# Where the operands of TensorE start in SBUF: stationary buffers on multiples of 64 bytes, ring slots 16 bytes further apart

## The reference

```python
h = x + 0.5 * swiglu(norm(x), w_ffn1_in, w_ffn1_out)         # d_ff 5632
z = norm(h) @ w_mix_in                                        # 5 groups of 1024 columns: B, C, H, U, V
y_conv = B * causal_dwconv3(C * H)
y_gm   = U * (tril(w_spatial[head]) @ norm(V) + b_spatial)
h = h + concat(y_conv, y_gm) @ w_mix_out
h = h + cross_attention(norm(h), norm(mem), w_xq, w_xk, w_xv, w_xo)   # 4 heads, 256 memory tokens
h = h + 0.5 * swiglu(norm(h), w_ffn2_in, w_ffn2_out)
out = norm(h)
```

## Time and profile before

| what | value |
|---|---|
| median of three runs | 2189.96 us |
| profiled execution, span from first to last instruction | 2187.2 us |
| TensorE busy with matmuls | 2167.1 us, 99% |
| VectorE busy | 1349.3 us, 62% |
| ScalarE busy | 991.6 us, 45% |
| DMA from and to HBM | mean 188 GB/s |

### The profile page before, as it was taken

One profiled execution on the slowest core, in us unless ns is written; L12 is line 12 of the kernel. 1 busy time (PEld: TensorE's weight loads), 2 busy tenths in 40 slices (PEclk: granted clock), 3 DMA queues, 4 the chain that ended last, 5 costly groups with the idle time before them and its releaser, 6 DMA issues.

```text
span 2187.2 us, 25558 instructions
## 1 busy us (share of the span) xinstructions
PE 2167.1 (99%) x9626; PEld 1778.9 (81%) x9626; DVE 1349.3 (62%) x1549; ACT 991.6 (45%) x1103; POOL 1.8 (0%) x7
## 2 busy tenths in 40 slices
PE   8999999999999999999999999999999999999998
PEld 6888888888888888888888888888888888888886
DVE  5676667666474547865677554576676667664544
ACT  5444454444343444444554444454444444443433
POOL 0000000000000000000000000000000000000000
PEclk9999999999999999999999999999999999999999
DMA  6666666665556565665556445466666666665553
GB/s 227 209 190 197 195 191 188 197 195 189 188 171 204 181 191 181 195 227 175 180 170 207 155 159 169 157 212 197 193 191 193 192 192 190 195 194 187 188 188 135
DMA packets 159217, 412.20 MB, mean 188 GB/s; under 512 B 12588, under 2 KB 13732, under 8 KB 158756
## 3 DMA queue, kind: packets, MB, share of 16 engines
q1 hardware_dynamic: 157728, 410.04, 60.2%
q10 hardware_dynamic: 1412, 1.11, 0.2%
HBM read 409.01 MB, written 2.10 MB: 188 GB/s over the span
## 4 chain that ended last, share of the span: by engine, by line
PE 96%; DVE 2%; ACT 1%; DMA 0%; issue 0%; ACTq 0%; DVEq 0%
PE ps L906 94%; PE ps L935 1%; DVE w_lo L575 1%; PE ps L919 1%; DVE ps L635 1%; DVE convT L748 0%; DVE xT_lo L583 0%; DMA h<-in_x 0%; ACT convT L444 0%; PE ps L1023 0%; ACT xT_hi L329 0%; ACT w_hi L321 0%; DVE stage L738 0%; ACT scratch L555 0%; ACT zT L441 0%
## 5 line engine op out<-in xcount | busy, mean ns | idle before, releaser
L575 DVE TENSOR_TENSOR w_lo<-raw,w_hi 128x1024 fp32r<-128x1024 f32 x768 | 936.1, 1224 | 773.8 <-ACT w_hi L321 768.6
L321 ACT ACTIVATE w_hi<-raw 128x1024 fp32r<-128x1024 f32 x768 | 811.8, 1061 | 1106.0 <-PE ps L906 1087.0
L906 PE MATMUL ps<-w_hi,xT_hi 128*128 128x512 f32 x1856 | 573.8, 390 | 5.3 <-DVE w_lo L575 5.3
L906 PE MATMUL ps<-w_lo,xT_hi 128*128 128x512 f32 x1856 | 572.2, 389 | 0.0
L906 PE MATMUL ps<-w_hi,xT_lo 128*128 128x512 f32 x1856 | 572.0, 389 | 0.0
L906 PEld LDWEIGHTS ps<-w_hi,xT_hi 128*128 128x128 f32 x1856 | 347.8, 188 | 78.9 <-issue 4.1
L906 PEld LDWEIGHTS ps<-w_lo,xT_hi 128*128 128x128 f32 x1856 | 349.0, 188 | 72.7
L906 PEld LDWEIGHTS ps<-w_hi,xT_lo 128*128 128x128 f32 x1856 | 348.7, 188 | 72.8
L906 PE MATMUL ps<-w_hi,hidT_hi 128*128 128x512 f32 x704 | 223.5, 397 | 0.4 <-DVE w_lo L575 0.4
L906 PE MATMUL ps<-w_hi,hidT_lo 128*128 128x512 f32 x704 | 222.7, 395 | 0.0
L906 PE MATMUL ps<-w_lo,hidT_hi 128*128 128x512 f32 x704 | 221.3, 393 | 0.0
(11 more groups left out here) (119 smaller groups left out, 800.7 us busy)
## 6 DMA issues: line engine op xcount, KB each, us to landing
raw<-in_w_ffn_in SPq DMA_DIRECT2D x352, 512.0 KB, 4.1
raw<-in_w_ffn_out SPq DMA_DIRECT2D x176, 512.0 KB, 4.3
raw<-in_w_mix_in SPq DMA_DIRECT2D x80, 512.0 KB, 4.2
raw<-in_w_mix_out SPq DMA_DIRECT2D x32, 512.0 KB, 3.7
raw<-in_w_xq SPq DMA_DIRECT2D x32, 512.0 KB, 3.8
raw<-in_w_xk SPq DMA_DIRECT2D x32, 512.0 KB, 3.9
raw<-in_w_xv SPq DMA_DIRECT2D x32, 512.0 KB, 3.6
raw<-in_w_xo SPq DMA_DIRECT2D x32, 512.0 KB, 3.6
```

The source lines that it names most:

```text
L321: nc.scalar.activation(w_hi[:, k % RING, :], raw[:, k % RAW, :], ACT.Copy).then_inc(hi_ready, 1)
L575: nc.vector.tensor_tensor(w_lo[:, k % RING, :], raw[:, k % RAW, :], w_hi[:, k % RING, :].bitcast(F32), ALU.subtract).then_inc(lo_ready, 1)
L906: ins = nc.tensor.matmul(bank(s, t * GW + b * BLK, BLK), xs[:, k, t * P:(t + 1) * P], ws_[:, k % RING, b * BLK:(b + 1) * BLK], start=(k == ...
```

## The change

`put` takes a `row`: the tensor then starts at a byte that is 64 * `row` past a multiple of 512. `xT_hi` gets row 0 and `xT_lo` row 4. `extra` is rounded up to a multiple of 64, and with it everything that lies on `extra` and `big`. The rings `w_hi` and `w_lo` become one flat tensor each, in which a slot is 1024 columns and the next slot starts 1028 columns (4112 bytes) further: `w_hi` starts on row 0, `w_lo` on row 4. The three places that use a slot take `w_hi[k % RING]` instead of `w_hi[:, k % RING, :]`.

| tensor | start before: byte, remainder by 64, by 512 | start after |
|---|---|---|
| `xT_hi` | 32896, 0, 128 | 33280, 0, 0 |
| `xT_lo` | 49280, 0, 128 | 49920, 0, 256 |
| `w_hi` slots 0 to 3 | remainders 0, 0, 0, 0 by 64 | 0, 16, 32, 48 by 64 |
| `w_lo` slots 0 to 3 | remainders 0, 0, 0, 0 by 64 | 0, 16, 32, 48 by 64 |
| `hidT_hi`, `yT_hi` | 137504, 32, 288 | 138752, 0, 0 |
| `pT_hi` | 129312, 32, 288 | 130560, 0, 0 |
| `v_hi` | 203040, 32, 288 | 204288, 0, 0 |

The instructions of every engine, their order and their waits stay as they are; only addresses differ.

```diff
--- before.py
+++ after.py
@@ -103,21 +103,33 @@
     KB = 1024
     place = {"at": BASE}
 
-    def put(name, shape, dt, at=None):
+    LINE = 64
+    PITCH = 512
+
+    def lines(at, row):
+        return at + (row * LINE - at) % PITCH
+
+    def put(name, shape, dt, at=None, row=None):
         size = 4
         for s in shape[1:]:
             size *= s
         if at is None:
-            at = place["at"]
-            place["at"] = at + (size + 31) // 32 * 32
+            at = (place["at"] + 31) // 32 * 32
+            if row is not None:
+                at = lines(at, row)
+            place["at"] = at + size
         return nc.alloc_sbuf_tensor_at(name, shape, dt, offset=at)
 
+    def put_ring(name, dt, skew, row):
+        ring = put(name, [P, RING * (GW + skew)], dt, row=row)
+        return [ring[:, i * (GW + skew):i * (GW + skew) + GW] for i in range(RING)]
+
     h = put("h", [P, TOK, D], F32)
-    xT_hi = put("xT_hi", [P, KD, SEQ], F32R)
-    xT_lo = put("xT_lo", [P, KD, SEQ], F32R)
+    xT_hi = put("xT_hi", [P, KD, SEQ], F32R, row=0)
+    xT_lo = put("xT_lo", [P, KD, SEQ], F32R, row=4)
     raw = put("raw", [P, RAW, GW], F32)
-    w_hi = put("w_hi", [P, RING, GW], F32R)
-    w_lo = put("w_lo", [P, RING, GW], F32R)
+    w_hi = put_ring("w_hi", F32R, LINE // 16, 0)
+    w_lo = put_ring("w_lo", F32R, LINE // 16, 4)
     stage = put("stage", [P, TOK, GW], F32)
     scratch = put("scratch", [P, GW], F32)
     ident = put("ident", [P, P], F32)
@@ -135,7 +147,7 @@
     nbias = put("nbias", [P, 4], F32)
     rsum = put("rsum", [P, 4], F32)
     rinv = put("rinv", [P, 4], F32)
-    extra = place["at"]
+    extra = (place["at"] + LINE - 1) // LINE * LINE
     g_v = put("g_v", [P, GW], F32, at=extra)
     ws = put("ws", [P, HEADS, P], F32, at=extra + 4 * KB)
     pT_hi = put("pT_hi", [P, XA_HEADS * 2, SEQ], F32R, at=extra)
@@ -159,7 +171,7 @@
     pT_lo = put("pT_lo", [P, XA_HEADS * 2, SEQ], F32R, at=big + 80 * KB)
     qT_hi, qT_lo = yT_hi, yT_lo
     kT_hi, kT_lo = xT_hi, xT_lo
-    assert big + 2 * KF * KB <= nc.sbuf_usable_end
+    assert big + 2 * KF * KB <= nc.sbuf_usable_end, (big + 2 * KF * KB, nc.sbuf_usable_end)
 
 
     vectors = [("g_ffn1", g_ffn1[0], KD), ("g_mix", g_mix[0], KD), ("g_xattn", g_xattn[0], KD), ("g_mem", g_mem[0], KD),
@@ -318,7 +330,7 @@
                     act.wait_ge(raw_loaded[k % RAW], unit0 * (16 // RAW) + 16 * (k // RAW + 1))
                     if not (isinstance(unit0, int) and unit0 + k < RING):
                         act.wait_ge(unit_used, unit0 + (k - RING + 1))
-                    nc.scalar.activation(w_hi[:, k % RING, :], raw[:, k % RAW, :], ACT.Copy).then_inc(hi_ready, 1)
+                    nc.scalar.activation(w_hi[k % RING], raw[:, k % RAW, :], ACT.Copy).then_inc(hi_ready, 1)
 
             def hi_scaled(dst, k0, g, s, name, b0=0, b1=4):
 
@@ -572,7 +584,7 @@
             def lo_units(unit0, k0, k1):
                 for k in range(k0, k1):
                     dve.wait_ge(hi_ready, unit0 + (k + 1))
-                    nc.vector.tensor_tensor(w_lo[:, k % RING, :], raw[:, k % RAW, :], w_hi[:, k % RING, :].bitcast(F32),
+                    nc.vector.tensor_tensor(w_lo[k % RING], raw[:, k % RAW, :], w_hi[k % RING].bitcast(F32),
                                             ALU.subtract).then_inc(lo_ready, 1)
 
             def lo_scaled(dst, hi, k0, g, s, name, b0=0, b1=4):
@@ -904,7 +916,7 @@
                         for xs, ws_ in ((T_hi, w_hi), (T_hi, w_lo), (T_lo, w_hi)):
                             for b in range(2) if only is None else only[1:]:
                                 ins = nc.tensor.matmul(bank(s, t * GW + b * BLK, BLK), xs[:, k, t * P:(t + 1) * P],
-                                                       ws_[:, k % RING, b * BLK:(b + 1) * BLK],
+                                                       ws_[k % RING][:, b * BLK:(b + 1) * BLK],
                                                        start=(k == 0 and xs is T_hi and ws_ is w_hi),
                                                        stop=(k == n - 1 and xs is T_lo))
                     if only is None:
```

## The result

The changed kernel takes 2212.7 us (median of four runs, 2212.0 to 2213.9) against 2190.0 us before. The ratio is 1.0104, with a 95% interval of 1.009 to 1.0118. It is slower by 22.8 us, where 2166 us was forecast, with a range up to 2208 us. The profiled executions stand 24.9 us apart, 2212.1 against 2187.2 us.

A forecast was written before the change was run, and what follows sets the result against it. TensorE was taken to bound the kernel through the time between matmul starts. The profiled 2187.2 us minus 24.3 for level stationary buffers, other terms 0, gave 2162.9; the runs' 2.8 us offset made 2165.7, forecast 2166 us, range 2156 to 2208.

The forecast's parts named there:

- What bounds the kernel: Whole kernel: TensorE, busy 99%, sets the time through 9216 matmuls at line 906 times the distance between starts.
- Stationary buffers on multiples of 64: hidT, yT and memT stages: 3648 matmuls go from 233.3 to 226.7 ns, saving 24.3 us.
- Ring slots: Streamed w_hi, w_lo: shifting 6912 matmuls' streams taken as 0; bounds +46.1 us and, at 213.3 ns each, -92 us.
- What is late next: ScalarE, VectorE and loads keep up when a unit of 12 matmuls takes 2.72 us; no cost.
- the shifted slots for ScalarE and VectorE: Their writes 16 to 48 bytes past a multiple stay hidden, even at half as much again on ScalarE's 1061 ns.
- Rows 0 and 4: Stationary `_hi` beside `w_lo` 256 bytes off: taken as 0, bounded by 6.67 ns on the matmuls concerned.
- The slower rival: Line 906, slots other than 0: distance between both tiles counts; 2199 us, or 2212 to 2214 us; chance 0.33.
- half price: Slower case's slots 1 and 3: 3.33 ns on each of 4608 matmuls, 15.4 us, giving 2199 us.
- full price: Slower case's slots 1 and 3 charged 6.67 ns a matmul like slot 2, giving 2212 to 2214 us.
- No change: Whole kernel: effects cancel, or streams are free and remainder by 64 is irrelevant; within 0.2% of 2190 us; chance 0.14.
- the cheaper stream: Line 906: shifted streams remove half of the 13.3 ns excess on 6912 matmuls, -46 us, 2120 us; chance 0.08.
- Lines of 16 bytes: SBUF addresses: all remainders start on a 16-byte line, so by that rule nothing moves and time stays 2190 us.

The follow-up runs named there:

- base32: The kernel before with all buffers placed 32 bytes further; 2189.7 us, ratio 1.0.
- align_only: The changed kernel without the 16-byte skew of the ring slots, all slots on multiples of 64; 2175.2 us, ratio 0.9932.
- all_level: The kernel before with `extra` rounded so hidT, yT, memT and pT share the rings' remainder by 256; 2166.5 us, ratio 0.9895.
- const48: The changed kernel without skew, every slot of both rings 48 bytes past a multiple of 64; 2223.2 us, ratio 1.014.

## Why the prediction was wrong

**What bounds the kernel** was right. TensorE stayed at 99% and its wait for `w_lo` at 5.8 us; in the twelve kernels of the experiments that wait lies between 4.8 and 6.0 us, so what moved their times is the time between matmuls.

**Stationary buffers on multiples of 64: 24.3 us saved.** The size was right and the reason wrong. Put level with the rings modulo 256, these 3648 matmuls give 23.1 us in the runs (2189.6 against 2166.5) and 22.6 in the spans. But what counts is not their remainder by 64: `base32` gives it to them and saves nothing, `align_only` saves 15 us because its buffers land at a distance of 64. Before, the distance was 96, from remainders of 128 and 288 by 512. Those stood in the table of the change; I read them by 64 because the change speaks of 64. The reason given, three buffers at different addresses with one and the same time, was weaker than it read: `hidT_hi` and `yT_hi` both start at byte 137504, and all three share the remainder by 512, so they were one case and not three. That 24.3 us came out right is luck in part: rounding to 64 alone gave 15 us in `align_only`.

**Ring slots: cost taken as 0.** This is the step that failed. It cost 47.5 us, 2212.1 against the 2164.6 us of `all_level`, where everything is level. That is over my upper bound of 46.1 us. The slots are at distances 0, 16, 32 and 48; held steady, the last three stand 5.0 to 6.6 ns over 226.7, and slot 0, which the bound took as free, pays too. The 0 came from rows of 256 columns, 119.7 against 120.0 ns. These are equal although one pair is level and the other at a distance of 96, as the `hidT` matmuls are, which differ by 6.7 ns from level ones at 512 columns. The two distances that the kernel before offers at 256 columns, 0 and 96, happen to cost the same there; 64, 128 and 224 are 1.2 to 2 ns cheaper. So the price at 256 columns is not the price at 512, in size or in sign, and why they differ stays open. The durations, 280/283/283 against 279/282/286, were the row that told of a difference, and I had it in the rival.

**What is late next, and the shifted slots for ScalarE and VectorE.** Right: 1062 and 1224 ns a unit after, against 1061 and 1224, and `all_level` holds 2.72 us a unit in every stage, with TensorE waiting 5.7 us for `w_lo`.

**Rows 0 and 4: cost taken as 0.** Right, 256 bytes being a whole period.

**The slower rival** named the mechanism, the distance between the tiles, with a period of 64 where the runs show 256; it took `hidT` for a distance of 32, and it was at 96. It gave 2199 us at half price and 2212 to 2214 at full price for slots 1 and 3. I took the half because nothing was known of 16 and 48, and gave the case 0.33. The total came out at the full price, but not its terms. By the averages on `xT`, slots 1 and 3 stand 4.8 and 6.0 ns over 226.7, which is 24.9 us on 2304 matmuls each, between the half (15.4) and the full price (30.7). Slot 0 was too small: four disturbed matmuls at 3.3 ns, 2.5 us, were put in, and there are ten, 3.7 ns over the whole unit, 8.5 us. The two misses cancel, so that 2212 was met is luck to that extent.

**No change and the cheaper stream** did not come. No distance tried went under 226.7 ns at 512 columns; at 256 columns three did go under the level one, by 1.2 to 2 ns.

**Lines of 16 bytes.** The Trainium skill, "SBUF — State Buffer", section Specifications (TRN2), gives SBUF lines of 16 bytes; by the reading of the prediction all starts on multiples of 16 would be alike. The runs disagree with that reading: 16 bytes cost 5.0 ns a matmul and 256 bytes cost none.

## What to carry to other kernels

When matmuls that load their stationary tile anew each time follow each other without a wait, look at the time between two starts, not at busy time, and compare it between buffers: two levels at equal shape (here 226.7 and 233.3 ns) are a reason to suspect the addresses, and moving one buffer tests it. For float32r matmuls of 512 columns, place all stationary and all streamed buffers on the same remainder by 256 bytes; here that is one line and 96 bytes of SBUF for 1.05% of the time. A cost of one shape (512 columns) must not be priced from another (256): here it had another size and another sign. And agreement between buffers that share an address is one observation, not several.

## What the runs showed of the hardware

- The time between the starts of float32r matmuls of 512 columns depends on (streamed start - stationary start) modulo 256 bytes. It is 226.7 ns at 0 and averages 228.9 to 233.3 over a stage at the eight other distances tried. The starts by themselves don't matter, as far as tried (`base32`).
- Off level, the byte distance does not fix the beat: 64 showed 228.9 and 233.3 ns, 48 showed 233.3 and 230.0, each in one trace, and whole runs of `const48` differ by 10 us. What chooses is open.
- Matmuls of 256 columns are 119.7 to 120.0 ns apart at 0 and 96, and 117.9 to 118.6 at 64, 128 and 224.
- The cost is not an equal amount on each matmul but a beat. At a distance of 96 the starts are 232, 237, 231 ns apart, over and over; at 16 they are 235, 230, 228, 234. At the level distance a disturbed sequence runs at 225 to 235 ns for up to ten matmuls before it stands at 226.7 (slot 0 of the changed kernel). There, one unit in four is level, and only its last two matmuls are on the beat.
- Also the best of these, 226.7 ns, lies above the 213.3 ns of the prediction's lower bound, and no run shows why. That the load of the next stationary tile meets the stream in SBUF is a guess that no run tested: every matmul here loads its stationary tile anew.
